# High weights times high and low input as one product of 512 columns in the MLPs

## The chip, the core and the metric

The kernel runs on one core of one Trainium2 chip. The metric is the device time of one execution in microseconds (us), the median over the runs of a kernel. Each core has a matrix engine (TensorE, PE in the rows, its weight loads as PEld), three engines for elementwise work (VectorE, DVE in the rows; ScalarE, ACT; GpSimd, POOL), and a queue (SP) that here issues the weight transfers. TensorE writes its products to an accumulator memory, PSUM: 8 banks of 512 fp32 values per partition, over 128 partitions.

## The reference, cut to what matters

Two layers over x of shape (1, 256, 2048). Each layer has a mixer (layer 0: a state-space part and a retention part; layer 1: latent attention) and then a gated MLP with a short convolution. The change touches the MLPs only:

```python
def conv_ffn(hn, w_up, conv_w, conv_b, w_down):
    a = hn @ w_up                       # 2048 -> 2 x 5632
    ap = jnp.pad(a, ((0, 0), (CONV_WIDTH - 1, 0), (0, 0)))
    a = ap[:, :-2] * conv_w[0] + ap[:, 1:-1] * conv_w[1] + ap[:, 2:] * conv_w[2] + conv_b
    gate, val = jnp.split(a, 2, axis=-1)
    return (jax.nn.silu(gate) * val) @ w_down
...
for layer in range(DEPTH):
    ...
    h = h + conv_ffn(rms_norm(h, ln_ffn[layer]), ffn_w_up[layer], ...)
```

All inputs and outputs are fp32.

## The kernel before, in words

**Split products.** Activations lie transposed, 128 features on the partitions and the T = 256 tokens along the row. A product with an fp32 weight matrix is made of three products in the reduced format fp32r (the rows print it as f32 on TensorE). Each operand is written as high part plus low part: `hi` is the weight rounded to fp32r by ScalarE (L370), `lo` is `raw - hi`, made by VectorE (L761). The input has both parts side by side in one row of 512: columns 0 to 255 high, columns 256 to 511 low (`XS` for the up projections, `YF` for the down projections). For each 128x128 weight tile the kernel adds up high weight by high input (L1548), high weight by low input (L1549) and low weight by high input (L1552), all into the first 256 columns of a PSUM bank:

```python
def by_high(bank, wh, x, first):
    mm(PS[:, bank, 0:T], wh, x[:, 0:T], start=first, stop=False)
    mm(PS[:, bank, 0:T], wh, x[:, T:2 * T], start=False, stop=False)
```

The second half of each such bank is not used. Every matmul instruction comes with its own weight load, also the second of two with the same weights.

**Pieces and steps.** Weights stream from memory through 4 `raw` slots; two pieces come with one transfer. A piece is the part of a transfer that is split at once into one of 4 slots of `hi` and `lo`. In an up projection a piece is 8 tiles (4 along k, 2 output tiles `ft`): first 16 high products, then 8 low ones (`std_piece`). A step is 4 pieces and fills a pair of banks, one per output tile. Two pairs of banks (`pair(e)`, banks 0 to 3) are used in turn. In a down projection a piece has 6 or 5 tiles of one output tile and a step is 8 pieces (`down`, L1783).

**An MLP** (`feed_forward`) goes through the hidden width in two halves. A half is 22 up steps in 11 blocks of two (first gate, then value columns), then 8 down steps. After a gate or value step VectorE takes the bank pair out, multiplies by the row norm and writes `apad` (`scale_banks`, L810), which frees the banks (`bank_free`). GpSimd convolves the gate columns. For the value columns ScalarE starts the convolution (L575) and VectorE ends it (L1140). ScalarE applies SiLU (L584), VectorE multiplies gate by value (`hid`, L1146), ScalarE rounds to `YF` high (L592), VectorE subtracts for `YF` low (L1154). After a down step VectorE adds the bank pair to the residual `H` (`add_residual`, L773).

**Order.** Each engine runs its own instruction list strictly in order and the lists are written out by hand; semaphores tie them. TensorE needs, before a piece, its `hi` (`hi_ready`), before the low products its `lo` (`lo_ready`), and before a step the pair of banks freed by the step two before. ScalarE may split piece p once piece p - 4 is done on TensorE (`piece_done`). On VectorE and ScalarE the steps of a block stand between the splits: in a block ScalarE and VectorE split the 4 pieces of the next step, and then VectorE takes out the banks of the step just done. The splits of the following pieces stand behind the convolution, SiLU and rounding of the block. In the last block of a half two of those splits stand between its parts. The first down step takes, for each of two output tiles, 6 and 5 of the first 11 rows of `YF` (pieces 0 to 3), and then 6 and 5 of the last 11 (pieces 4 to 7). So before its piece 5, the sixth, TensorE waits for `YF` low of the last block (`hl_ready`, L1792).

Of the kernel before, what the change touches and what calls it, by code (L numbers as in the profile page):

```python
# [20 lines left out]
P = 128  # L21
T = 256
# [14 lines left out]
SLOTS = 4  # L37
# [28 lines left out]
def build(nc, A, out):  # L66
# [6 lines left out]
    with ctx:  # L73
# [103 lines left out]
        XF = sb("XF", [P, KD, T], fp32, ffn)  # L177
        ffn.close()
# [145 lines left out]
        hl_ready = sem("hl_ready")  # L324

# [33 lines left out]
        def _(act):  # L359
# [197 lines left out]
            def feed_forward(layer, n, p0, e0):  # L557

                for half in range(2):
# [3 lines left out]

                    def up(r, j0, kinds, first, last=False):
                        q = p + 8 * j0
                        if first:
                            first_step(n, q + 4)
                        else:
                            splits(q + 4, 8, r)
                        splits(q + 8, 8, r, kinds)  # L570

# [182 lines left out]
        def _(dve):  # L754
# [13 lines left out]
            def add_residual(p_end, e, sp_, se, r, j0, n=None):  # L768
# [3 lines left out]
                h = H[:, 2 * j0:2 * j0 + 2, :] if r is None else H[:, ds(r * 4 + 2 * j0, 2), :]  # L772
                V.tensor_tensor(h, h, PS[:, b:b + 2, 0:T], ALU.add).then_inc(bank_free, 1)  # L773
# [32 lines left out]
            def scale_banks(d, p_end, e, sp_=0, r=None):  # L806
# [3 lines left out]
                V.tensor_tensor(d, PS[:, b:b + 2, 0:T], rn2, ALU.mult).then_inc(bank_free, 1)  # L810

# [304 lines left out]
            def feed_forward(layer, n, p0, e0):  # L1116
                for half in range(2):
# [4 lines left out]
                    def up(r, j0, kinds, first, last=False):  # L1122
# [8 lines left out]
                        scale_banks(apad[:, 0, :, 2:T + 2], q + 4, e + 2 * j0, 8, r)  # L1131
                        splits(q + 8, 8, r, kinds)
                        scale_banks(apad[:, 1, :, 2:T + 2], q + 8, e + 2 * j0 + 1, 8, r)
# [30 lines left out]
                    add_residual(q + 8, ed, 0, 0, None, 0, m)  # L1164
                    with dve.Fori(0, 3) as r:
                        for i in (1, 2):
                            splits(q + 8 * i + 4, 16, r, ("down",) * 8)
                            add_residual(q + 8 * i + 8, ed + i, 16, 2, r, i, m)
# [5 lines left out]
                    add_residual(q + 64, ed + 7, 0, 0, None, 7, m)  # L1174
# [364 lines left out]
        def _(pe):  # L1539
# [10 lines left out]

            def by_low(bank, wl, x, last):
                return mm(PS[:, bank, 0:T], wl, x[:, 0:T], start=False, stop=last)  # L1552
# [4 lines left out]
            def std_piece(p, i, bank, mov, s=0, r=None, nk=4, pieces=4):  # L1557

                pe.wait_ge(hi_ready, at(p + 1, s, r))
                for ft in range(2):  # L1560
                    for k in range(nk):
                        kk = i * nk + k
                        wh, _ = tile(p, k, nk, ft * P)
                        by_high(bank + ft, wh, mov(kk), kk == 0)
# [7 lines left out]
            def step(p, e, mov, s=0, se=0, r=None, before=None, after=None):  # L1572
# [3 lines left out]
                for i in range(4):  # L1576
                    if before:
                        before(i)
                    std_piece(p + i, i, pair(e), mov, s, r)
# [188 lines left out]
            def feed_forward(layer, n, p0, e0):  # L1768
                for half in range(2):
# [3 lines left out]
                    if half == 0:  # L1773
                        step(p, e, XSk, before=x_split(n), after=lambda i: norm_sum(n) if i == 2 else None)
                    else:
                        step(p, e, XSk)
                    step(p + 4, e + 1, XSk)
                    with pe.Fori(0, GS // 2) as r:
                        for j in range(4):
                            step(p + 8 + 4 * j, e + 2 + j, XSk, 16, 4, r)  # L1780
# [281 lines left out]
```

## Time and profile before

| what | value |
|---|---|
| median of 3 runs | 2176.58 us (2176.45 to 2183.63) |
| profiled execution, its own time | 2176.14 us |
| its span, first to last instruction | 2174.3 us |
| mean granted TensorE clock over the span | 0.997 |
| busy share: PE / DVE / ACT / POOL | 99% / 68% / 47% / 29% |
| matmul instructions | 18496 |
| memory read | 395.23 MB, 183 GB/s over the span |

How to read it: "busy" of TensorE is the time in which at least one matmul was in the pipeline, so 99% says that it hardly ever stood still, not that it ran at its peak. The other engines have room on average; what counts is whether their work is ready at the moment TensorE asks for it. In a timeline row the first number is the start in us from the span's start, the second the length in us, and the end of the row says how many instructions of the kind were merged. A single matmul lasts longer than the distance to the next one, because they overlap in the pipeline; the distance between starts is what it costs.

### The profile page before, as it was taken

How to read it: one execution, taken by the hardware profiler on the slowest of the kernel's cores; microseconds unless marked ns; L12 is line 12 of the kernel's file. 1: busy time of each engine (PE TensorE's matmuls, PEld its weight loads, DVE VectorE, ACT ScalarE, POOL GpSimd, SP SyncE). 2: the span in 40 equal slices, each digit the busy share in tenths (PEclk: the TensorE clock that was granted, in tenths of full speed). 3: DMA queues.
4: the chain of work that ended last, by engine and by line, in shares of the span. 5: the costliest groups of instructions: out<-in, count | busy, mean ns of one | idle time of the engine just before them, and what ended most of it. 6: DMA issues, size and time to landing. Idle time of an engine off the chain costs nothing.

```text
span 2174.3 us, 47266 instructions
## 1 busy us (share of the span) xinstructions
PE 2143.2 (99%) x18496; PEld 2120.6 (98%) x18496; DVE 1469.3 (68%) x1808; ACT 1028.0 (47%) x1338; POOL 632.7 (29%) x628
## 2 busy tenths in 40 slices
PE   8999999999999999999999999999999999999997
PEld 8999999999999999999999999999999999999997
DVE  6798895777666556666666667677665555666665
ACT  5455544444444444444444455445444444444443
POOL 4644430234343003434211111233434003343311
PEclk9999999999999999999999999999999999999999
DMA  6444444555554665555556444555554565555553
GB/s 256 176 161 160 159 170 144 200 191 199 187 199 152 210 212 194 197 189 197 169 190 227 145 141 143 186 186 196 194 192 170 191 208 206 192 194 190 168 197 118
DMA packets 67154, 399.91 MB, mean 184 GB/s; under 512 B 9776, under 2 KB 11696, under 8 KB 31600
## 3 DMA queue, kind: packets, MB, share of 16 engines
q1 hardware_dynamic: 60192, 391.15, 50.5%
q10 hardware_dynamic: 5712, 6.21, 0.9%
q8 instruction: 70, 1.15, 0.2%
q0 software_dynamic: 1152, 1.18, 0.2%
q14 instruction: 28, 0.23, 0.0%
HBM read 395.23 MB, written 2.10 MB: 183 GB/s over the span
## 4 chain that ended last, share of the span: by engine, by line
PE 94%; DVE 2%; ACT 1%; issue 1%; DVEq 1%; DMA 0%; POOL 0%; POOLq 0%; ACTq 0%
PE PS L1548 29%; PE PS L1552 29%; PE PS L1549 29%; PE PS L1707 1%; PE PS L1709 1%; PE PS L1708 1%; PE PS L1673 1%; DVE lo L761 1%; ACT hi L370 0%; PE PS L1914 0%; PE PS L1915 0%; PE PS L1928 0%; PE PS L1659 0%; PE PS L1901 0%; PE PS L1898 0%
## 5 line engine op out<-in xcount | busy, mean ns | idle before, releaser
L761 DVE TENSOR_TENSOR lo<-raw,hi 128x1024 fp32r<-128x1024 f32 (+2 forms) x826 | 950.5, 1170 | 498.5 <-ACT hi L370 493.5
L370 ACT ACTIVATE hi<-raw 128x1024 fp32r<-128x1024 f32 (+2 forms) x826 | 786.6, 970 | 744.2 <-PE PS L1552 700.1
L1548 PE MATMUL PS<-XS,hi 128*128 128x256 f32 x3600 | 847.5, 278 | 8.6 <-ACT hi L370 8.6
L1549 PE MATMUL PS<-XS,hi 128*128 128x256 f32 x3600 | 842.5, 277 | 0.0
L1548 PEld LDWEIGHTS PS<-XS,hi 128*128 128x128 f32 x3600 | 677.7, 188 | 11.9 <-issue 11.5
L1549 PEld LDWEIGHTS PS<-XS,hi 128*128 128x128 f32 x3600 | 677.4, 188 | 0.4
L1552 PE MATMUL PS<-XS,lo 128*128 128x256 f32 x3600 | 483.5, 277 | 0.0
L1552 PEld LDWEIGHTS PS<-XS,lo 128*128 128x128 f32 x3600 | 443.6, 188 | 0.0
L1549 PE MATMUL PS<-YF,hi 128*128 128x256 f32 x1408 | 331.8, 276 | 0.0
L1548 PE MATMUL PS<-YF,hi 128*128 128x256 f32 x1408 | 331.7, 276 | 0.0
L1497 POOL TENSOR_TENSOR ctmp<-apad,cws 128x512 f32<-128x512 f32 x88 | 131.9, 1520 | 524.7 <-DVE apad L810 524.7
L1548 PEld LDWEIGHTS PS<-YF,hi 128*128 128x128 f32 x1408 | 264.3, 188 | 0.0
L1549 PEld LDWEIGHTS PS<-YF,hi 128*128 128x128 f32 x1408 | 264.3, 188 | 0.0
L1552 PE MATMUL PS<-YF,lo 128*128 128x256 f32 x1408 | 201.2, 276 | 0.0
L1552 PEld LDWEIGHTS PS<-YF,lo 128*128 128x128 f32 x1408 | 178.6, 188 | 0.0
L1346 POOL TENSOR_TENSOR sq<-H 128x512 f32 x31 | 33.1, 1066 | 407.2 <-DVE H L773 407.2
L1140 DVE SCALAR_TENSOR_TENSOR cvo<-apad,cws,cvo 128x256 f32<-128x256 f32 x176 | 77.6, 482 | 50.5 <-ACT cvo L575 46.8
L1504 POOL TENSOR_TENSOR cvo<-cvo,ctmp 128x512 f32<-128x512 f32 x44 | 90.3, 2053 | 6.3
L1499 POOL TENSOR_SCALAR cvo<-apad,cws 128x256 f32<-128x256 f32 x88 | 91.5, 1047 | 0.0
L1492 POOL COPY cws<-cw 128x16 f32 (+1 forms) x44 | 10.9, 249 | 271.8 <-DVE hid L1146 251.9
L575 ACT ACTIVATE cvo<-apad,cws 128x256 f32<-128x256 f32 x88 | 48.2, 595 | 85.6 <-DVE apad L810 85.6
L592 ACT ACTIVATE YF<-hid 128x512 f32 (+1 forms) x44 | 27.9, 633 | 96.9 <-DVE hid L1146 96.9
(260 smaller groups left out, 2267.9 us busy)
## 6 DMA issues: line engine op xcount, KB each, us to landing
raw<-in_ffn_up SPq DMA_DIRECT2D x176, 1024.0 KB, 4.8
raw<-in_ffn_dn SPq DMA_DIRECT2D x128, 704.0 KB, 4.1
raw<-in_w_in SPq DMA_DIRECT2D x51, 1024.0 KB, 4.8
raw<-in_w_oe SPq DMA_DIRECT2D x16, 1024.0 KB, 4.8
raw<-in_w_oo SPq DMA_DIRECT2D x16, 1024.0 KB, 4.8
raw<-in_mla_dn SPq DMA_DIRECT2D x9, 1024.0 KB, 4.8
raw<-in_w_ukv SPq DMA_DIRECT2D x8, 1024.0 KB, 5.2
raw<-in_w_uq SPq DMA_DIRECT2D x8, 768.0 KB, 4.3
```

Source lines behind the costliest of these rows:

```text
L370: act.activation(hi[:, p % SLOTS, 0:n], raw[:, u % SLOTS, off:off + n], ACT.Copy).then_inc(hi_ready, 1)
L575: ins = act.activation(cvo[:, 1, t, :], apad[:, 1, t, 2:T + 2], ACT.Identity, bias=cws[:, 4 * t + 11:4 * t + 12], scale=cws[:, 4 * t + 10: ...
L592: act.activation(dh, hid[:, :, :], ACT.Copy).then_inc(hh_ready, 1)
L761: V.tensor_tensor(lo[:, p % SLOTS, 0:n], raw[:, u % SLOTS, off:off + n], f(hi[:, p % SLOTS, 0:n]), ALU.subtract).then_inc(lo_ready, 1)
L1140: V.scalar_tensor_tensor(out=cvo[:, 1, t, :], in0=apad[:, 1, t, i:T + i], scalar=cws[:, 8 + 4 * t + i:9 + 4 * t + i], in1=cvo[:, 1, t, :], ...
L1346: G.tensor_tensor(sq[:, :, :], h, h, ALU.mult)
L1497: G.tensor_tensor(ctmp[:, i, :, :], apad[:, 0, :, i:T + i], w(i), ALU.mult)
L1499: G.tensor_scalar(cvo[:, 0, t, :], apad[:, 0, t, 2:T + 2], cws[:, 4 * t + 2:4 * t + 3], cws[:, 4 * t + 3:4 * t + 4], ALU.mult, ALU.add)
L1504: G.tensor_tensor(cvo[:, 0], cvo[:, 0], ctmp[:, 0], ALU.add).then_inc(cv_ready, 1)
L1548: mm(PS[:, bank, 0:T], wh, x[:, 0:T], start=first, stop=False)
L1549: mm(PS[:, bank, 0:T], wh, x[:, T:2 * T], start=False, stop=False)
L1552: return mm(PS[:, bank, 0:T], wl, x[:, 0:T], start=False, stop=last)
```

## The change

In the up and down projections of both MLPs the two high products become one over all 512 columns of the input row, into the whole bank: columns 0 to 255 hold high by high, and, as before, low by high is added there; columns 256 to 511 hold high by low. The mixers keep the two products.

After an up step ScalarE copies the second halves of the two banks to a new buffer `low` (it waits for the step's last piece and for the previous banks to be free) and signals `half_ready`; VectorE adds the first halves to `low`, drains, and multiplies by the norm into `apad`. After a down step VectorE adds the second halves to `H`, drains, and then adds the first halves.

```diff
+        low = sb("low", [P, 2, T], fp32, ffn)
+                    def low_half(r, p_end, e_):
+                        act.wait_ge(piece_done, at(p_end, 8, r))
+                        act.wait_ge(bank_free, at(e_, 2, r))
+                        b = pair(e_)
+                        act.activation(low[:, :, :], PS[:, b:b + 2, T:2 * T], ACT.Copy).then_inc(half_ready, 1)
...
                             splits(q + 4, 8, r)
+                        low_half(r, q + 4, e + 2 * j0)
                         splits(q + 8, 8, r, kinds)
+                        low_half(r, q + 8, e + 2 * j0 + 1)
...
+                if wide:
+                    V.tensor_tensor(h, h, PS[:, b:b + 2, T:2 * T], ALU.add)
+                    dve.drain()
                 V.tensor_tensor(h, h, PS[:, b:b + 2, 0:T], ALU.add).then_inc(bank_free, 1)
...
+            def scale_halves(d, count, e, r):
+                dve.wait_ge(half_ready, at(count, 2, r))
+                b = pair(e)
+                V.tensor_tensor(low[:, :, :], low[:, :, :], PS[:, b:b + 2, 0:T], ALU.add)
+                dve.drain()
+                V.tensor_tensor(d, low[:, :, :], rn2, ALU.mult).then_inc(bank_free, 1)
...
-                        scale_banks(apad[:, 0, :, 2:T + 2], q + 4, e + 2 * j0, 8, r)
+                        scale_halves(apad[:, 0, :, 2:T + 2], 2 * (s0 + j0) + 1, e + 2 * j0, r)
                         splits(q + 8, 8, r, kinds)
-                        scale_banks(apad[:, 1, :, 2:T + 2], q + 8, e + 2 * j0 + 1, 8, r)
+                        scale_halves(apad[:, 1, :, 2:T + 2], 2 * (s0 + j0) + 2, e + 2 * j0 + 1, r)
...
+            def by_high_wide(bank, wh, x, first):
+                mm(PS[:, bank, :], wh, x, start=first, stop=False)
...
-                                by_high(pair(ed + i0) + ft, hi[:, pc % SLOTS, k * P:(k + 1) * P], YF[:, kk + k, :], kk + k == 0)
+                                by_high_wide(pair(ed + i0) + ft, hi[:, pc % SLOTS, k * P:(k + 1) * P], YF[:, kk + k, :], kk + k == 0)
```

`step` and `std_piece` take the function for the high products as an argument; all up steps of the MLPs pass `by_high_wide`, and the three `add_residual` calls of the MLPs (first down step, the six in a loop, the last) pass `wide`.

## Rows read from the trace of the kernel before

**Rows 1.** The page: engines' busy time (us, share of the span, instructions).
```profile
PE 2143.2 (99%) x18496; PEld 2120.6 (98%) x18496; DVE 1469.3 (68%) x1808; ACT 1028.0 (47%) x1338; POOL 632.7 (29%) x628
```

**Rows 2.** The page: the chain that ended last, by engine.
```profile
PE 94%; DVE 2%; ACT 1%; issue 1%; DVEq 1%; DMA 0%; POOL 0%; POOLq 0%; ACTq 0%
```

**Rows 3.** The waits of TensorE: us in total, times, longest; two longest and last of eleven.
```profile
PE PS L1548 <- ACT hi L370: 8.6, 1, 8.6
PE PS L1928 <- ACT C L679: 3.5, 7, 0.5
...
PE PS L1922 <- DVE C L1278: 0.4, 1, 0.4
```

**Rows 4.** Busy time by stretch, with TensorE clock and DMA share.
```profile
core 0: us, PE busy (x) PEld busy (x) DVE busy (x) ACT busy (x) POOL busy (x), PEclk, DMA share, GB/s
...
620.00:830.00 210.00, 210.00 (x1856) 210.00 (x1855) 121.98 (x140) 93.48 (x114) 34.64 (x28) 1.00 0.57 195
```

**Rows 5.** Groups by line over the MLPs of layer 0 (457 to 1175 us).
```profile
L1548 PE MATMUL PS<-XS,hi 128*128 128x256 f32 x1405 | 327.4, 276 | 0.0
...
L1548 PE MATMUL PS<-YF,hi 128*128 128x256 f32 x704 | 165.9, 276 | 0.0
```

**Rows 6.** Timeline, TensorE, steady stretch of an up projection (low products).
```profile
570.24 1.07 PE L1552 MATMUL PS<-XS,lo 128*128 128x256 f32 x8
...
572.96 1.07 PE L1552 MATMUL PS<-XS,lo 128*128 128x256 f32 x8
...
575.67 1.07 PE L1552 MATMUL PS<-XS,lo 128*128 128x256 f32 x8
```

**Rows 7.** Timeline, weight loads (PEld) beside products (PE).
```profile
500.42 0.28 PE L1548 MATMUL PS<-XS,hi 128*128 128x256 f32 x1
500.54 0.28 PE L1549 MATMUL PS<-XS,hi 128*128 128x256 f32 x1
500.65 0.28 PE L1548 MATMUL PS<-XS,hi 128*128 128x256 f32 x1
...
500.43 0.19 PEld L1549 LDWEIGHTS PS<-XS,hi 128*128 128x128 f32 x1
500.54 0.19 PEld L1548 LDWEIGHTS PS<-XS,hi 128*128 128x128 f32 x1
```

**Rows 8.** Timeline, weight loads of plain fp32 operands.
```profile
16.68 1.60 PEld L1610 LDWEIGHTS PS<-S,ones 128*128 128x128 f32 x8
```

**Rows 9.** The chain, start of the kernel: products of plain fp32 operands.
```profile
16.96 1.73 PE PS L1610 x8
```

**Rows 10.** Groups by line: nearest operations to the added ones.
```profile
L773 DVE TENSOR_TENSOR H<-H,PS 128x512 f32 x36 | 24.5, 680 | 0.0
...
L688 ACT ACTIVATE KN<-PS 128x512 f32<-128x512 f32 x8 | 4.8, 598 | 11.5 <-PE PS L1901 11.5
```

**Rows 11.** The instructions on apad: ns minimum, median, maximum.
```profile
L810 DVE TENSOR_TENSOR apad<-PS,rn x88: 677/683/685, 471.8 to 2041.2; 128x512 f32<-128x512 f32 x88
```

**Rows 12.** Timeline, ScalarE and VectorE in the steady block of rows 6.
```profile
573.27 2.94 ACT L370 ACTIVATE hi<-raw 128x1024 fp32r<-128x1024 f32 x3
...
568.14 0.68 DVE L810 TENSOR_TENSOR apad<-PS,rn 128x512 f32<-128x512 f32 x1
...
574.35 4.75 DVE L761 TENSOR_TENSOR lo<-raw,hi 128x1024 fp32r<-128x1024 f32 x4
```

**Rows 13.** Timeline, first block of layer 0: ScalarE, VectorE, then TensorE.
```profile
487.32 3.89 ACT L370 ACTIVATE hi<-raw 128x1024 fp32r<-128x1024 f32 x4
...
480.02 2.27 DVE L761 TENSOR_TENSOR lo<-raw,hi 128x1024 fp32r<-128x1024 f32 x1 [1.40 <-ACT hi L370]
...
488.40 3.50 DVE L761 TENSOR_TENSOR lo<-raw,hi 128x1024 fp32r<-128x1024 f32 x3 [0.26 <-ACT hi L370]
...
489.54 0.28 PE L1548 MATMUL PS<-XS,hi 128*128 128x256 f32 x1
```

**Rows 14.** Timeline, end of the first up projection: VectorE, then TensorE.
```profile
698.04 0.68 DVE L810 TENSOR_TENSOR apad<-PS,rn 128x512 f32<-128x512 f32 x1
...
704.85 0.69 DVE L1154 TENSOR_TENSOR YF<-hid,YF 128x512 fp32r<-128x512 f32 x1
...
705.10 0.84 PE L1552 MATMUL PS<-YF,lo 128*128 128x256 f32 x6
705.78 0.28 PE L1548 MATMUL PS<-YF,hi 128*128 128x256 f32 x1
```

**Rows 15.** Timeline, end of the kernel.
```profile
2159.29 0.69 DVE L773 TENSOR_TENSOR H<-H,PS 128x512 f32<-128x512 f32 x1 [5.82 <-PE PS L1552]
2160.01 0.63 ACT L736 ACTIVATE sums<-H 128x512 f32<-128x512 f32 x1 [7.41 <-DVE H L773]
```

More of the change, by code:

```diff
@@ L324, in build @@
         hl_ready = sem("hl_ready")
+        half_ready = sem("half_ready")
         odd_loads = sem("odd_loads")
@@ L766, in splits, with add_residual @@
                     split(p + i, s, r, k)
-            def add_residual(p_end, e, sp_, se, r, j0, n=None):
+            def add_residual(p_end, e, sp_, se, r, j0, n=None, wide=False):
                 dve.wait_ge(piece_done, at(p_end, sp_, r))
@@ L1163, in feed_forward @@
                     splits(q + 6, kinds=("down",) * 6)
-                    add_residual(q + 8, ed, 0, 0, None, 0, m)
+                    add_residual(q + 8, ed, 0, 0, None, 0, m, True)
                     with dve.Fori(0, 3) as r:
@@ L1167, in feed_forward @@
                             splits(q + 8 * i + 4, 16, r, ("down",) * 8)
[L1168 removed]
+                            add_residual(q + 8 * i + 8, ed + i, 16, 2, r, i, m, True)
                     splits(q + 60, kinds=("down",) * 4)
@@ L1173, in feed_forward @@
                         splits(q + 64, kinds=("std",) * 3)
-                    add_residual(q + 64, ed + 7, 0, 0, None, 7, m)
+                    add_residual(q + 64, ed + 7, 0, 0, None, 7, m, True)
                     if half == 1 and n < 3:
@@ L1555, in piece, with std_piece @@
                 pe.wait_ge(lo_ready, at(p + 1, s, r))
-            def std_piece(p, i, bank, mov, s=0, r=None, nk=4, pieces=4):
+            def std_piece(p, i, bank, mov, s=0, r=None, nk=4, pieces=4, high=by_high):
                 pe.wait_ge(hi_ready, at(p + 1, s, r))
@@ L1563, in std_piece @@
                         wh, _ = tile(p, k, nk, ft * P)
-                        by_high(bank + ft, wh, mov(kk), kk == 0)
+                        high(bank + ft, wh, mov(kk), kk == 0)
                 piece(p, s, r)
@@ L1570, in std_piece, with step @@
                 ins.then_inc(piece_done, 1)
-            def step(p, e, mov, s=0, se=0, r=None, before=None, after=None):
+            def step(p, e, mov, s=0, se=0, r=None, before=None, after=None, high=by_high):
                 if e >= 2:
@@ L1578, in step @@
                         before(i)
-                    std_piece(p + i, i, pair(e), mov, s, r)
+                    std_piece(p + i, i, pair(e), mov, s, r, high=high)
                     if after:
@@ L1773, in feed_forward @@
                     if half == 0:
-                        step(p, e, XSk, before=x_split(n), after=lambda i: norm_sum(n) if i == 2 else None)
+                        step(p, e, XSk, before=x_split(n), after=lambda i: norm_sum(n) if i == 2 else None, high=by_high_wide)
                     else:
-                        step(p, e, XSk)
-                    step(p + 4, e + 1, XSk)
+                        step(p, e, XSk, high=by_high_wide)
+                    step(p + 4, e + 1, XSk, high=by_high_wide)
                     with pe.Fori(0, GS // 2) as r:
                         for j in range(4):
-                            step(p + 8 + 4 * j, e + 2 + j, XSk, 16, 4, r)
+                            step(p + 8 + 4 * j, e + 2 + j, XSk, 16, 4, r, high=by_high_wide)
                     q, ed = p + UPP, e + 2 * GS
```

## The prediction

> **What bounds the kernel now.** First the page's busy times [rows 1]: TensorE is busy 99% of the span, VectorE 68%, ScalarE 47%. Then the chain that ended last [rows 2]: 94% of it is TensorE. A busy TensorE could still be one that waits in small gaps, so next its waits [rows 3]: eleven kinds, from one of 8.6 us at the very start down to 0.4, about 22 us together, and none of them more than one wait on a high or low product. In a down projection [rows 4] TensorE is busy for all of 210.00 us at a granted clock of 1.00, the upper level of 2.4 GHz, while the DMA engines are at 0.57. So the MLPs last as long as their matmul instructions stand apart, and the reader has to find that distance. The low products of consecutive pieces start at 570.24, 572.96 and 575.67 [rows 6]: 2.72 us for a piece of 24 instructions, 113.3 ns each. 256 columns at 2.4 GHz are 106.7 ns, so an instruction costs 6.7 ns over its columns.
>
> **What the change takes from TensorE.** The MLP of layer 0 has 1408 first high products on XS (three records are missing) and 704 on YF [rows 5]; layer 1 has the same. That makes 2 x 2112 = 4224 pairs that become one instruction each. A pair costs 2 x 113.3 = 226.7 ns now. The columns stay the same (213.3 ns), so the question is only what an instruction of 512 columns costs beyond them, and no row shows one. The bounds:
>
> - Nothing is won if the 6.7 ns go with the columns: 226.7 ns.
> - One fixed cost of 6.7 ns is won if it goes with the fp32r instruction: 220.0 ns.
> - More is won if the weight load sets today's distance. In the rows each weight load starts with the product before it, and the next product starts 0.11 us after the load [rows 7]: load and product take turns, both about 0.11 us long, and one cannot say from these rows which one waits. The nearest row with time to spare for the load are plain fp32 products near the start: 8 of them in 1.73 us, 216 ns each [rows 9], and their 8 loads are just as long (1.60 us for 8, the last one 0.19) [rows 8]. By their distance such an instruction keeps the array busy for twice its 256 columns, so 512 column times, and costs 3 ns over them.
>
> I take 216 ns. It is the only row where the array is held for 512 column times, and there the weight load of about 0.11 us is hidden as it would be here. Saved per pair 10.7 ns; times 4224 is 45.2 us. The other ends: 6.7 ns x 4224 = 28.2 us, and 0. The low products behind keep 113.3 ns. The last of them still hides the load for the next wide product.
>
> The Trainium skill says on "TensorE: Matmul & The Clock Gate", in "LDWEIGHTS (loading the stationary operand)", that a load takes its columns at 1.2 GHz. For 128 columns that is 106.7 ns, as an estimate, and it would make the load the slower part of today's turn; rows 7 do not contradict it. The same page's section "Back-to-back issue gap" gives N/2.4 + 2.5 ns for an isolated product, 109.2 ns for 256 columns and 215.8 for 512. The 113.3 ns of the trace do not agree with the first, the 216 ns of the fp32 rows agree with the second. By the page alone the pair would win 2.6 ns, and all of them 11 us.
>
> **What it adds, and where that lies.** An up step gets a ScalarE copy of 128x512 from PSUM (598 ns, L688) and a VectorE addition of 128x512 with one operand in PSUM (680 ns, L773) [rows 10]; the multiplication that follows now reads `low` and stays at about 683 ns [rows 11]. A down step gets one more addition of 680 ns. With a drain I count 0.75 us for VectorE each time (estimate: 0.68 plus 0.07, the step between two operations across a drain). The copy is hidden: it runs on ScalarE behind the split of the step's last piece, while VectorE subtracts that same piece for 1.2 us. In all VectorE gets 88 + 32 times 0.75 = 90 us more, ScalarE 88 x 0.60 = 53 us; at 68% and 47% that fits.
>
> What matters is latency at four places.
>
> - *The steady block.* The first split behind a block's convolution is ready at 574.35, where VectorE starts to subtract it; the chain of the block opens with the evacuation at 568.14 [rows 12]. TensorE wants that piece at 575.67 + 8 x 0.113 = 576.58 [rows 6]. Slack 2.2 us. From it go about 0.25 us for signal and weight load, 0.75 for the new addition, and 0.34 because TensorE runs 4 pieces of 8 pairs in between, 10.7 ns faster each. 0.9 us are left: nothing is paid.
> - *The first block of a layer.* A table load makes it later. The split is there at 488.40, TensorE starts it at 489.54 [rows 13]: 1.14 us. Less 0.25, 0.75 and 0.34 this is -0.2: 0.2 us of waiting, twice, 0.4 us.
> - *The end of an up projection.* The chain evacuation (698.04), convolution, SiLU, `YF` low ends at 704.85 + 0.69 = 705.54, and the piece that waits for it starts at 705.78 [rows 14]. The 0.24 us are just signal and weight load, so the slack is about nil. With 0.75 us more in the chain, and TensorE earlier by 28 pairs x 10.7 ns = 0.30 us, TensorE stands for 1.05 us. This comes four times: 4.2 us. What is late next is nothing: the splits of the following pieces shift with the chain and TensorE has stood by then.
> - *The end.* The last residual addition (2159.29, 0.69 us) is followed by the sum of squares (2160.01) that all of the final norm waits for [rows 15]: 0.75 us more. The other 31 residual additions lie beside 14 us of a down step, and the squares and the next layer's input have three pieces (8 us) of time.
>
> Sum: -45.2 + 0.4 + 4.2 + 0.75 = -39.9 us. Against the profiled execution's own 2176.14 us that is 2136.2; the median of the runs shown is 0.44 higher, so about 2137.
>
> **The rivals.**
>
> - *A fixed cost goes with each fp32r instruction* (220.0 ns). For it: the 6.7 ns are steady over every MLP piece, and the fp32 rows are of another format. Against it: it needs a cost twice as large as in the fp32 rows. Then 28.2 us are won; the stand at the end of an up projection is 0.75 + 0.19 = 0.94 us, four times 3.8, the first blocks cost 0.1, the end 0.75: 2176.6 - 23.6 = 2153.
> - *The cost goes with the columns, the change does not do what it says* (226.7 ns). Nothing is won, 0.75 us are lost at four ends and at the last: 3.75 us, 2180. Against it: 256 columns at 2.4 GHz explain 106.7 of 113.3 ns, and a rate of 2.26 columns a ns is neither clock level.
> - *VectorE's chain stops TensorE in every block.* This is the one on the slow side. The place is the first split behind each of 44 blocks; it decides from 1.65 us of added latency on (2.2 - 0.25 - 0.34). The row that speaks for it is a split stretched to 2.27 us where others take 1.2, at a time when GpSimd works [rows 13]. If the two new steps and the split before them all stretch by that 1.05 us, the chain grows by 0.75 + 3.15 = 3.9 us, TensorE stands 2.25 us in each block, 99 us, and the time is 2137 + 99 = 2236. It is slower than before by over 0.5% from about 2.8 us on. Against it: none of the 88 evacuations took over 685 ns [rows 11], and the new addition reads the same PSUM and writes as much.
> - *Products overlap beyond their columns.* The same page's section "Back-to-back issue gap" also gives about 131 ns for a sustained 512-column product. As a mechanism here: wide products would start before the columns of the one ahead are through. 226.7 - 131 = 95.7 ns x 4224 would take off up to 404 us before another engine stops it, at best 1772. No row here has 256 columns in less than 107 ns.
>
> **How the numbers follow.** 216 ns a pair: 0.67. 220 ns: 0.18. Columns: 0.08. VectorE's chain in every block: 0.04 with a loss, 0.02 with a part of the gain left. Overlap: 0.01. About 0.5%, 11 us, is what a measurement of this kernel can tell from no change, so the borders are 2165.7 and 2187.5. Faster: 0.67 + 0.18 + 0.02 + 0.01 = 0.88. Same: 0.08. Slower: 0.04. The predicted time is the likeliest case, 2137. Its own range is 2132 (no standing at the up ends) to 2142 (standing twice as long). The range given reaches to the 220 ns case, 2155, and holds 0.85.
>
> **What would show it.** In the trace after: wide products 0.216 us apart and a piece of an up projection in 8 x 0.216 + 8 x 0.113 = 2.63 us in place of 2.72; at 220 ns it is 2.67, at 226.7 it stays at 2.72. TensorE's waits should name four waits of about a microsecond on `YF` of L1154 at the first down step of each half, and two of a few tenths on the `hi` split in the first block of each layer. L810 should stay at 683 ns and the addition before it take 680. The final chain should be 0.75 us longer from the last product on. The prediction is wrong if the wide product takes another time than 216 ns, or if TensorE waits for `hi` in the blocks of the loops.

## The result and the profile after

The change makes the kernel slower: 2213.68 us median (2213.12 to 2220.03, 4 runs) against 2176.93 (2176.45 to 2183.63, 4 runs) on the same chip, ratio 1.0179, 95% interval 1.0165 to 1.0194. Forecast were 2137 us, a range of 2132 to 2155, and a chance of 0.04 for slower. The profiled execution has a span of 2211.3 us, at a mean granted TensorE clock of 0.996.

The page of the kernel after, busy times; it answers to [rows 1]:

```profile
PE 2175.3 (98%) x14272; PEld 1962.8 (89%) x14272; DVE 1575.6 (71%) x1928; ACT 1065.1 (48%) x1426; POOL 653.8 (30%) x628
```

The 4224 instructions are gone (18496 to 14272) and TensorE is busy 32 us longer. The waits of TensorE after (us in total, times, longest), two rows, against [rows 3]:

```profile
PE PS L1570 <- ACT hi L372: 8.3, 1, 8.3
...
PE PS L1574 <- ACT hi L372: 2.9, 4, 1.0
```

On the products of the MLPs only the four waits at L1574, the wide product, are new, 2.9 us together. The waits in the mixers and at the end differ by up to 1 us each. So the loss is not standing time. Busy time of the same stretch as [rows 4]:

```profile
core 0: us, PE busy (x) PEld busy (x) DVE busy (x) ACT busy (x) POOL busy (x), PEclk, DMA share, GB/s
620.00:830.00 210.00, 209.53 (x1204) 182.39 (x1203) 135.02 (x154) 97.02 (x122) 35.86 (x28) 1.00 0.55 190
```

The clock is at its upper level of 2.4 GHz (1.00), the DMA share is no higher than before. What is left is the distance between products. The timeline of TensorE in the steady stretch, against [rows 6] (L1574 the wide product, L1577 the low one):

```profile
566.58 2.02 PE L1574 MATMUL PS<-XS,hi 128*128 128x512 f32 x8
568.44 1.07 PE L1577 MATMUL PS<-XS,lo 128*128 128x256 f32 x8
569.35 2.02 PE L1574 MATMUL PS<-XS,hi 128*128 128x512 f32 x8
571.21 1.07 PE L1577 MATMUL PS<-XS,lo 128*128 128x256 f32 x8
572.12 2.02 PE L1574 MATMUL PS<-XS,hi 128*128 128x512 f32 x8
```

From 566.58 to 568.44 there are 8 wide products: 232.5 ns each, where the prediction took 216. The 8 low ones from 568.44 to 569.35 take 113.8 ns each. A piece lasts 2.77 us, where it was 2.72. The single starts in the trace show a pattern that comes back in nearly every piece of an up projection: 226, 236, 231, 236, 231, 236, 231, 236 ns, then 118 for the first low product and 113 to 114 for the rest. In the down projections it is mostly 233 to 234 in the pieces of six tiles and 226 to 236 in those of five. The low products behind are no longer at 113.3 ns either: their mean over the trace is 114.0 ns in the up projections and 116.4 in the down projections.

The two instructions that VectorE has in an up step after (ns minimum, median, maximum), against [rows 11]:

```profile
L832 DVE TENSOR_TENSOR apad<-low,rn x88: 691/693/1041, 471.4 to 2073.3; 128x512 f32<-128x512 f32 x88
```
```profile
L830 DVE TENSOR_TENSOR low<-low,PS x88: 672/677/682, 470.7 to 2072.5; 128x512 f32<-128x512 f32 x88
```

The addition is as forecast (680). The multiplication was thought to stay at 683 and is up to 1041 ns long. In the trace 24 of its 88 instances take 1023 to 1041 ns, and these are the 24 that lie beside an instruction of GpSimd; the other 64 take 691 to 694. Of the 88 additions 26 lie beside GpSimd, and they take 672 to 680 ns like the rest. VectorE in the steady block, against [rows 12]: split, addition, multiplication, and the first split behind the block; then the instruction of GpSimd that lies beside them:

```profile
567.87 1.22 DVE L772 TENSOR_TENSOR lo<-raw,hi 128x1024 fp32r<-128x1024 f32 x1 [1.27 <-ACT hi L372]
569.01 0.68 DVE L830 TENSOR_TENSOR low<-low,PS 128x512 f32<-128x512 f32 x1
569.76 1.03 DVE L832 TENSOR_TENSOR apad<-low,rn 128x512 f32<-128x512 f32 x1
...
576.31 1.23 DVE L772 TENSOR_TENSOR lo<-raw,hi 128x1024 fp32r<-128x1024 f32 x1
```
```profile
567.90 2.34 POOL L1526 TENSOR_TENSOR cvo<-cvo,ctmp 128x512 f32<-128x512 f32 x1
```

From the first step of the evacuation to that split it was 6.21 us (568.14 to 574.35), now it is 7.30 (569.01 to 576.31): 1.09 more, 0.75 for the addition and 0.34 for the longer multiplication. TensorE begins the piece at 577.67, 1.36 us after (it was 2.2): slack is left, nothing is paid there.

The end of the first up projection, VectorE and TensorE, against [rows 14]:

```profile
709.25 0.69 DVE L1176 TENSOR_TENSOR YF<-hid,YF 128x512 fp32r<-128x512 f32 x1
```
```profile
708.76 0.85 PE L1577 MATMUL PS<-YF,lo 128*128 128x256 f32 x6
710.08 1.40 PE L1574 MATMUL PS<-YF,hi 128*128 128x512 f32 x5 [0.47 <-ACT hi L372]
```

Six low products should take 0.69 us and took 1.32: TensorE stands for 0.63 us. The row names the split of ScalarE, but what came last is `YF` low (709.25 + 0.69 = 709.94, 0.14 us before the piece). This is one of the four waits above. The end of the kernel, against [rows 15]:

```profile
2194.31 0.69 DVE L785 TENSOR_TENSOR H<-H,PS 128x512 f32<-128x512 f32 x1 [6.02 <-PE PS L1577]
2195.07 0.69 DVE L787 TENSOR_TENSOR H<-H,PS 128x512 f32<-128x512 f32 x1
```

The second addition starts 0.76 us after the first.

**Where the 37 us are.** By the starts of products in the two traces, the up projection's second half (last product on `YF` to the next first one) lasts 244.18 us, was 239.47: 4.71 for 704 pairs. A down projection's half (first to last product on `YF`) lasts 123.4 or 124.0, was 119.57. Four up halves give 18.8 us and four down halves 16.5 (3.8 of it standing, as the experiment below shows by a down half of 122.75 without the new evacuation). The kernel's end, from the last product on `YF` to the last matmul, is 1.5 us longer. Together 36.8; the last matmul is 36.5 us later.

### The profile page after: what moved, and what is told of

Its sections match the earlier page's. It is cut to its first block, busy times and chain, and to the rows that moved or that the text cites. A ratio compares the mean times of both kernels' runs of the same rounds, so it can differ in the third digit from the quotient of the medians.

```text
span 2211.3 us, 39270 instructions
## 1 busy us (share of the span) xinstructions
PE 2175.3 (98%) x14272; PEld 1962.8 (89%) x14272; DVE 1575.6 (71%) x1928; ACT 1065.1 (48%) x1426; POOL 653.8 (30%) x628
## 3 DMA queue, kind: packets, MB, share of 16 engines
q10 hardware_dynamic: 5712, 6.21, 0.9%
## 4 chain that ended last, share of the span: by engine, by line
PE 93%; DVE 2%; ACT 2%; issue 1%; DVEq 1%; DMA 0%; POOL 0%; POOLq 0%; ACTq 0%
PE PS L1574 44%; PE PS L1577 28%; PE PS L1570 7%; PE PS L1571 7%; PE PS L1732 1%; PE PS L1734 1%; PE PS L1733 1%; DVE lo L772 1%; PE PS L1698 1%; ACT hi L372 1%; PE PS L1939 0%; PE PS L1940 0%; PE PS L1953 0%; PE PS L1684 0%; PE PS L1926 0%
## 5 line engine op out<-in xcount | busy, mean ns | idle before, releaser
L772 DVE TENSOR_TENSOR lo<-raw,hi 128x1024 fp32r<-128x1024 f32 (+2 forms) x826 | 969.5, 1197 | 419.7 <-ACT hi L372 415.8
L1574 PE MATMUL PS<-XS,hi 128*128 128x512 f32 x2816 | 712.8, 395 | 0.0
L1574 PEld LDWEIGHTS PS<-XS,hi 128*128 128x128 f32 x2816 | 503.2, 188 | 93.9
L1577 PEld LDWEIGHTS PS<-XS,lo 128*128 128x128 f32 x3600 | 471.8, 188 | 31.9
L1577 PE MATMUL PS<-XS,lo 128*128 128x256 f32 x3600 | 485.0, 277 | 0.0
L1574 PE MATMUL PS<-YF,hi 128*128 128x512 f32 x1408 | 369.2, 394 | 2.9 <-ACT hi L372 2.9
L1519 POOL TENSOR_TENSOR ctmp<-apad,cws 128x512 f32<-128x512 f32 x88 | 154.2, 1771 | 560.1 <-DVE apad L832 560.1
L1574 PEld LDWEIGHTS PS<-YF,hi 128*128 128x128 f32 x1408 | 245.5, 188 | 43.5 <-ACT hi L372 3.6
L1577 PEld LDWEIGHTS PS<-YF,lo 128*128 128x128 f32 x1408 | 201.3, 188 | 23.4
L1577 PE MATMUL PS<-YF,lo 128*128 128x256 f32 x1408 | 205.5, 279 | 0.0
L1570 PE MATMUL PS<-XS,hi 128*128 128x256 f32 x784 | 191.5, 285 | 8.3 <-ACT hi L372 8.3
L1571 PE MATMUL PS<-XS,hi 128*128 128x256 f32 x784 | 187.0, 280 | 0.0
L1570 PEld LDWEIGHTS PS<-XS,hi 128*128 128x128 f32 x784 | 148.8, 190 | 11.5 <-issue 11.2
L1571 PEld LDWEIGHTS PS<-XS,hi 128*128 128x128 f32 x784 | 148.8, 190 | 0.3
L1526 POOL TENSOR_TENSOR cvo<-cvo,ctmp 128x512 f32<-128x512 f32 x44 | 80.0, 1817 | 6.3
L1524 POOL TENSOR_TENSOR cvo<-cvo,ctmp 128x512 f32<-128x512 f32 x44 | 73.8, 1677 | 6.5
```

Of the source, the lines that this page charges most:

```text
L772: V.tensor_tensor(lo[:, p % SLOTS, 0:n], raw[:, u % SLOTS, off:off + n], f(hi[:, p % SLOTS, 0:n]), ALU.subtract).then_inc(lo_ready, 1)
L1519: G.tensor_tensor(ctmp[:, i, :, :], apad[:, 0, :, i:T + i], w(i), ALU.mult)
L1524: G.tensor_tensor(cvo[:, 0], cvo[:, 0], ctmp[:, 1], ALU.add)
L1526: G.tensor_tensor(cvo[:, 0], cvo[:, 0], ctmp[:, 0], ALU.add).then_inc(cv_ready, 1)
L1574: mm(PS[:, bank, :], wh, x, start=first, stop=False)
```

## The experiments

### Is it the wide product or the evacuation? A square of four

*Two products of 256 columns into the two halves, new evacuation* (`e1_two_halves`):

```diff
-                mm(PS[:, bank, :], wh, x, start=first, stop=False)
+                mm(PS[:, bank, 0:T], wh, x[:, 0:T], start=first, stop=False)
+                mm(PS[:, bank, T:2 * T], wh, x[:, T:2 * T], start=False, stop=False)
```

> The high products are two of 256 columns again, but into the two halves of the bank, and all of the new evacuation stays. Theory A (the 512-column product itself costs 226 to 236 ns, more than twice 113.3): products 113.3 ns apart as before, so 2177 plus the four stands at the ends of the up projections (0.75 us each) and 0.75 us at the end, about 2181. Theory B (the added copies and additions slow TensorE's stream, whatever its width): most of the 37 us stays, over 2205.

*Wide product, old evacuation* (`f1_wide_old_evac`). The second half of the bank is computed and never added:

```diff
-                        low_half(r, q + 4, e + 2 * j0)
...
-                        scale_halves(apad[:, 0, :, 2:T + 2], 2 * (s0 + j0) + 1, e + 2 * j0, r)
+                        scale_banks(apad[:, 0, :, 2:T + 2], q + 4, e + 2 * j0, 8, r)
...
-                    add_residual(q + 8, ed, 0, 0, None, 0, m, True)
+                    add_residual(q + 8, ed, 0, 0, None, 0, m)
```

> The wide products stay; the evacuation is that of the kernel before, and the second halves of the banks (high weight by low input) are never added. Theory A (the wide product itself costs 232.7 ns on average against 226.7 for two of 256): 4224 x 6 = 25 us over before and no stands at the ends of the up projections, about 2202, with the 226, 231 and 236 ns unchanged. Theory B (the later and heavier evacuation makes them slow): wide products at 226.7 or less throughout, about 2177.

*Both* (`f2_halves_old_evac`), the two edits together; it too never adds the second half:

> Two products of 256 columns into the two halves of the bank, evacuation as before, second halves never added. In the run with the new evacuation the products stood 113.3 ns apart in some halves and 117.6 in others; the change of rhythm came where a weight load had waited for its high weights, by then only 0.12 to 0.15 us ahead. Theory C (the late evacuation uses up the 2.3 us of slack, a load comes some ns late, and the stream stays in the slow rhythm): with the old evacuation the slack is back at 2.2 us, all products at 113.3 ns, 2177. Theory D (writing the second half of the bank brings the slow rhythm): stretches at 117.6 remain, over 2185.

| high products | evacuation | median us (runs) | ratio to before, 95% |
|---|---|---|---|
| wide | new (the change) | 2213.68 (4) | 1.0179 (1.0165 to 1.0194) |
| wide | old | 2210.50 (4) | 1.0148 (1.0131 to 1.0165) |
| two of 256 | new | 2199.85 (10, from 2187.66 to 2219.49) | 1.0102 (1.0068 to 1.0137) |
| two of 256 | old | 2176.81 (10, from 2174.43 to 2180.68) | 0.9996 (0.9985 to 1.0007) |

The wide product alone costs 2210.50 - 2176.81 = 33.7 us. In its trace the pattern of 226, 231 and 236 ns is unchanged, the up half is 244.18 us as in the change, the down half 122.75. Against two products of 256 columns (239.47 and 119.57 us) these are 4.71 us for 704 pairs, 6.7 ns a pair, and 3.18 us for 352, 9.0 ns a pair: about 6 ns on each wide product (mean 232.7), and the rest on the low products behind it. With the wide product the new evacuation adds 3.2 us; with two products of 256 it adds 23.0. The two costs don't add. The third row met neither of its forecasts (2181 and over 2205), its runs lie far apart, and it needs an explanation of its own.

### What of the wide product costs more than its columns?

Three experiments of one run each, with the new evacuation. *The same columns twice* (`e2_same_columns`): the wide product streams the 256 high columns two times (high by low is left out), so it reads a row of 1 KB and not of 2 KB.

```diff
-                mm(PS[:, bank, :], wh, x, start=first, stop=False)
+                xx = x[:, 0:T].unsqueeze(1).broadcast_to([P, 2, T])
+                mm(PS[:, bank, :].rearrange("p (a t) -> p a t", a=2), wh, xx, start=first, stop=False)
```

> The wide product streams the 256 high columns twice, so high weight by low input is left out. Theory A1 (the time goes with the columns that are streamed and written, not with what is read): wide products keep their 226, 231 and 236 ns, 2214. Theory A2 (reading a row of 2 KB is what is slow): they come down to about 226.7 or less, 2177 to 2190.

2215.29 us, distances unchanged (the same pattern, 232.5 ns in the steady stretch). Where the columns are read from is not it.

*Half the weights* (`e3_half_weights`): all wide products but the first of a bank use 64 weight columns (half of the outputs' high part is left out):

```diff
+                if first:
+                    mm(PS[:, bank, :], wh, x, start=first, stop=False)
+                else:
+                    mm(PS[0:64, bank, :], wh[:, 0:64], x, start=False, stop=False)
```

> All wide products but the first of each bank load 64 of 128 weight columns; the other half of their output is left out. Theory A3 (the weight load, which starts with each wide product, takes time from it): the load is half as long, and wide products come down from 232 towards 216 to 226 ns, a gain of 20 us or more against the kernel after, under 2195. Theory A1: no change of distance, 2214.

2218.4 us. The weight loads fall from 190 to 135 ns (two groups of its trace, 560 to 600 us), and the wide product stays at a mean of 231.9 ns (232.7 in the change), while the low ones of the up projections go from 114.0 to 116.8:

```profile
L1577 PEld LDWEIGHTS PS<-XS,hi 128*64 128x64 f32 x109 | 14.5, 135 | 8.0
L1575 PEld LDWEIGHTS PS<-XS,hi 128*128 128x128 f32 x6 | 1.1, 190 | 0.3
```

The length of the weight load is not it: with the load cut by 55 ns the wide product lost 0.8.

*384 and 128 columns* (`e4_384_128`), two products again:

```diff
+                mm(PS[:, bank, 0:384], wh, x[:, 0:384], start=first, stop=False)
+                mm(PS[:, bank, 384:512], wh, x[:, 384:512], start=False, stop=False)
```

> The 512 columns as a product of 384 and one of 128. If an fp32r product costs 17 column times for 16 columns (113.3 ns for 256, 226.7 for 512), the 384 columns take 170 ns and the 128 take 56.7 unless a weight load of about 110 ns sets the distance, which would make the pair 280 ns and the kernel about 2400 (2177 + 4224 x 0.053). If the load does not set it, 227 to 237 ns, 2180 to 2220.

2427.53 us, an up half of 280.54. Its timeline:

```profile
562.94 0.33 PE L1574 MATMUL PS<-XS,hi 128*128 128x384 f32 x1
563.11 0.22 PE L1575 MATMUL PS<-XS,hi 128*128 128x128 f32 x1
563.17 0.39 PE L1574 MATMUL PS<-XS,hi 128*128 128x384 f32 x1
563.40 0.22 PE L1575 MATMUL PS<-XS,hi 128*128 128x128 f32 x1
563.46 0.39 PE L1574 MATMUL PS<-XS,hi 128*128 128x384 f32 x1
```

The first 384 take 170 ns and the 128 behind them 60: they are near their columns at 2.4 GHz times 17/16 (170 and 56.7), like 256 in 113.3. So the 6.7 ns of an fp32r product do go with its columns. From then on a pair takes 0.29 us, 285 ns by the up half (227 and 58 more). The run had been forecast at 280 ns a pair and about 2400 us for the case that a weight load of about 110 ns does not fit behind a product of 128 columns, and it came out so: 113 + 170 = 283. That it is the load was not shown apart from this sum.

*Wide and low in turn* (`f3_interleaved`): each tile's wide and low product one after the other, new evacuation, in place of 8 wide ones and then 8 low ones.

```diff
+                        if high is by_high_wide:
+                            ins = by_low(bank + ft, wl, mov(kk), i == pieces - 1 and k == nk - 1)
```

> The kernel after, but each wide product is followed at once by the low product of the same tile, so no wide product follows another. The first wide product of each piece, which follows a low one, took 226 ns in the kernel after, the others 231 and 236. Theory E (the extra comes only where wide follows wide): wide 226.7, low 113 to 118, 4224 x 6 = 25 us less than the kernel after, 2185 to 2200. Theory F (every product over 256 columns pays it, whatever stands before): 230 to 236 stays, 2210 or more.

2246.79 us (4 runs), ratio 1.0316 (1.0299 to 1.0333). Now a wide product takes 235 ns and a low one 118 to 119:

```profile
563.10 0.28 PE L1577 MATMUL PS<-XS,lo 128*128 128x256 f32 x1
563.22 0.40 PE L1574 MATMUL PS<-XS,hi 128*128 128x512 f32 x1
563.46 0.28 PE L1577 MATMUL PS<-XS,lo 128*128 128x256 f32 x1
```

The edit also makes each piece of the up projections wait for its `lo` from the start; that is 2.7 us of waits in all. Changing the length at each step makes it worse, about 14 ns a pair over 17/16 of the columns in place of 6.7, so changes could be the cause of the whole extra. The next three test that, one run each. All have the old evacuation. *448 columns* (`g_448_columns`) and *320 columns* (`g_320_columns`) compute 64 and 192 columns of high by low less (what stands in the second half of a bank is not added in either):

```diff
-                mm(PS[:, bank, :], wh, x, start=first, stop=False)
+                mm(PS[:, bank, 0:448], wh, x[:, 0:448], start=first, stop=False)
```

> The wide product with the old evacuation, but over 448 of its 512 columns (64 columns of the high weights times the low input are left out). By columns x 17/16 at 2.4 GHz a product is 198.3 ns, 28.3 ns less than 226.7, so 4224 of them take 120 us off the 2176.8 of the two halves: 2057 us, and an up projection's half lasts 239.47 - 704 x 0.0283 = 219.5 us. If the extra 4 to 9 ns (226, 236, 231 in turn) come with every product longer than 256 columns, the distances are 198, 207, 203, the up half lasts 224 us and the time is about 2090. If they come only with a product that fills the bank (512), the distances are all 198 and the time is 2057.

> As the run with 448 columns, with 320 (192 columns of the high weights times the low input are left out). By the columns 141.7 ns a product. An up half of 239.47 - 704 x 0.085 = 179.6 us where nothing else stops TensorE, 184 us with 6 ns more for each product. VectorE, busy for about 1500 us, comes close to being late, so what is read here are the distances inside the pieces and not the total: all at 142 if only a full bank pays extra, 142 to 151 in turn if every product longer than 256 does. Total near 1820 if nothing waits, more where TensorE waits for the split.

*All products of the MLPs wide* (`g_all_wide`), the low one too; again the second half is not added:

```diff
+            def by_low_wide(bank, wl, x, last):
+                return mm(PS[:, bank, :], wl, x, start=False, stop=last)
```

> The wide product with the old evacuation, and the low product wide too (over both halves of the input; the second half of the bank is not read), so that the stream of the MLPs has products of one length only. If the extra nanoseconds come from the change of length between the wide and the low products, all stand 226.7 ns apart and the time is 2176.8 + 4224 x 0.1133 = 2655 us, an up half 239.47 + 704 x 0.1133 = 319.2 us. If each product of 512 columns costs 232.7 on the mean, it is 2655 + 8448 x 0.006 = 2706 us and an up half 327.7 us.

Timelines of the three, in this order (L1572 the high product, L1575 the low one, L1578 the wide low one):

```profile
564.87 1.78 PE L1572 MATMUL PS<-XS,hi 128*128 128x448 f32 x8
566.49 1.08 PE L1575 MATMUL PS<-XS,lo 128*128 128x256 f32 x8
567.41 1.78 PE L1572 MATMUL PS<-XS,hi 128*128 128x448 f32 x8
```
```profile
754.82 1.04 PE L1572 MATMUL PS<-YF,hi 128*128 128x320 f32 x6
755.70 0.87 PE L1575 MATMUL PS<-YF,lo 128*128 128x256 f32 x6
756.40 0.90 PE L1572 MATMUL PS<-YF,hi 128*128 128x320 f32 x5
```
```profile
562.95 2.03 PE L1578 MATMUL PS<-XS,lo 128*128 128x512 f32 x8
564.82 2.03 PE L1572 MATMUL PS<-XS,hi 128*128 128x512 f32 x8
566.68 2.03 PE L1578 MATMUL PS<-XS,lo 128*128 128x512 f32 x8
568.55 1.79 PE L1572 MATMUL PS<-XS,hi 128*128 128x512 f32 x7
```

448 columns: 1.62 us for 8, 202.5 ns, 4 over the 198.3 that 17/16 of the columns give; 2087.21 us, an up half of 223.63. The forecast of an extra for every length above 256 (224 us, about 2090) was right. 320 columns: 0.88 us for 6, 146.7 ns, 5 over the 141.7, with the low products at 116.7. The total there, 1958.95 us, is set by something else: TensorE waits 44 times for the `hi` split, 72.9 us in all, and in eleven stretches of the MLPs, 37.5 us together, its granted clock is 0.50. All wide: 5.60 us for 24, 233.3 ns each in every stretch of the MLPs; 2712.08 us where 2706 was forecast for this case and 2655 for the other. A stream of one length has 6.7 ns over 226.7 on every product, so the extra of the long product does not need a change of length. Changes add to it: the pair has 6.7 ns over 17/16 of its columns where the length changes every 8 products, 9.0 in the shorter pieces of the down projections, and about 14 where it changes each time.

### Why does the new evacuation cost 23 us with products of 256 columns?

The trace of `e1_two_halves` has no more waits than the change's, but a long stretch in which each product takes 117.7 ns and not 113.3. Low products of consecutive pieces, before and after the switch:

```profile
598.52 1.07 PE L1578 MATMUL PS<-XS,lo 128*128 128x256 f32 x8
```
```profile
657.10 1.10 PE L1578 MATMUL PS<-XS,lo 128*128 128x256 f32 x8
659.93 1.11 PE L1578 MATMUL PS<-XS,lo 128*128 128x256 f32 x8
662.76 1.10 PE L1578 MATMUL PS<-XS,lo 128*128 128x256 f32 x8
```

The last two steps are 2.83 us for 24 products, 117.9 ns (117.6 to 117.7 by the single starts); the step from 598.52 to the next low products (601.24) is 2.72, as before. The slow rhythm holds from 618.5 us on, and an up half in it lasts 248.86 us against 239.47. It sets in at one place. A stand of TensorE of 0.3 us at 707.4 us does not end it, one of 0.6 us at 1081 us does. VectorE, GpSimd, ScalarE, then TensorE where it sets in:

```profile
608.88 2.25 DVE L772 TENSOR_TENSOR lo<-raw,hi 128x1024 fp32r<-128x1024 f32 x1 [1.24 <-ACT hi L372]
611.05 0.67 DVE L830 TENSOR_TENSOR low<-low,PS 128x512 f32<-128x512 f32 x1
611.80 1.03 DVE L832 TENSOR_TENSOR apad<-low,rn 128x512 f32<-128x512 f32 x1
```
```profile
608.76 1.28 POOL L1524 TENSOR_TENSOR cvo<-cvo,ctmp 128x512 f32<-128x512 f32 x1
610.18 2.10 POOL L1526 TENSOR_TENSOR cvo<-cvo,ctmp 128x512 f32<-128x512 f32 x1
```
```profile
617.27 1.99 ACT L372 ACTIVATE hi<-raw 128x1024 fp32r<-128x1024 f32 x2
```
```profile
618.47 0.29 PE L1574 MATMUL PS<-XS,hi 128*128 128x256 f32 x1
618.59 0.28 PE L1575 MATMUL PS<-XS,hi 128*128 128x256 f32 x1
618.71 0.28 PE L1574 MATMUL PS<-XS,hi 128*128 128x256 f32 x1
```

The split in front of the evacuation takes 2.25 us in place of 1.22 and the multiplication 1.03 in place of 0.69, so with the addition the chain is late by 1.03 + 0.34 + 0.75 = 2.1 us, the whole slack. The `hi` that TensorE needs is ready at 618.33 (617.27 and 1.06 for one split), just when its weight load is due: the loads before are 113 ns apart and this one comes after 125, at 618.37. From the product at 618.47 on the starts are 0.12 us apart. No wait is listed. Two experiments ask whose lateness it is, and whether lateness alone does it.

*ScalarE's copy only* (`g_scalar_copy_only`): the copy and the wait for it stay, and VectorE multiplies out of PSUM as before (high by low is left out in the up steps; the down steps keep both additions):

```diff
-                V.tensor_tensor(low[:, :, :], low[:, :, :], PS[:, b:b + 2, 0:T], ALU.add)
-                dve.drain()
-                V.tensor_tensor(d, low[:, :, :], rn2, ALU.mult).then_inc(bank_free, 1)
+                V.tensor_tensor(d, PS[:, b:b + 2, 0:T], rn2, ALU.mult).then_inc(bank_free, 1)
```

> Two products of 256 columns into the two halves of a bank (2199.85 us with the whole new evacuation, 2176.8 with none), with ScalarE's copy and the wait for it kept in the up steps, but VectorE evacuating as before, one multiplication out of PSUM (the high weights times the low input are left out of the up steps; the down steps keep their addition). If VectorE's added step and its multiplication out of SBUF beside GpSimd's work are what made the split late, the slack behind a block is back near 2 us, the products keep 113.3 ns and the time is 2177 to 2181 us. If the copy or the wait for it is, the slack stays below 1 us and the time is near 2200.

2179.55 us (2175.38 to 2181.55, 10 runs), ratio 1.0012 (1.0002 to 1.0021). Its steady block, from evacuation to split:

```profile
567.40 0.68 DVE L830 TENSOR_TENSOR apad<-PS,rn 128x512 f32<-128x512 f32 x1
...
573.61 3.50 DVE L772 TENSOR_TENSOR lo<-raw,hi 128x1024 fp32r<-128x1024 f32 x3
```

6.21 us again, the slack back at 2.27, all MLP products at 113.3 ns, and an up half of 239.47. So the copy, the wait for it and the 32 additions of the down steps cost 2.6 us (0.4 to 4.6), and about 20 of the 23 are VectorE's added step and its multiplication out of SBUF. The two were not taken apart.

*A late ScalarE* (`f4_late_scalar`): the kernel before with four idle copies on ScalarE in each block, in front of the split:

```diff
+                        for k in (4, 5, 6):
+                            act.activation(PS[:, k, :].rearrange("p (a n) -> p a n", a=4), ones[:, :].unsqueeze(1).broadcast_to([P, 4, P]), ACT.Copy)
+                        act.activation(idle[:, :, :], ones[:, :].unsqueeze(1).broadcast_to([P, 4, P]), ACT.Copy)
```

> The kernel before with four idle ScalarE copies of 128x512 behind each of the 44 blocks of the up projections, which use up about 2.1 of the 2.27 us that the next high weights are ready ahead. Its products and its evacuation are untouched. Theory C (a weight load that comes some ns late turns the stream to the slow rhythm): stretches of products at 117.6 ns in the MLPs where the kernel before has none, up to 12672 x 4.3 ns = 54 us, 2185 to 2230. Theory D (the rhythm has nothing to do with waiting): 113.3 throughout and at most the waits themselves, below 2187.

2201.35 us. The split is ready 0.05 us before the piece is due and the up halves take 243.1 and 244.7 us. Most blocks pay in a gap; at 577.42 it is one product of 0.23 us:

```profile
577.42 0.38 PE L1552 MATMUL PS<-XS,hi 128*128 128x256 f32 x1
577.65 0.28 PE L1553 MATMUL PS<-XS,hi 128*128 128x256 f32 x1
```

The slow rhythm comes too (918 to 942 us and 1851 to 1898 us in this trace), but not behind most late splits; in `e1_two_halves` too the second layer keeps 113.3 ns with splits only 0.12 us early. So a late split can cost time with hardly a wait listed, and it can start the slow rhythm; it does not do so each time. What decides that stays open.

## Why the prediction was wrong, point by point

- **"I take 216 ns"**: this step failed, and with it the sum. The wide product measured 232.5 ns. Of this, 226.7 is the rival "the cost goes with the columns", which had a chance of 0.08 and a time of 2180 us: 128, 256 and 384 columns take 57 to 60, 113.3 and 170 ns. The rest, 6 ns on the mean, was in no rival; it comes with products of 320, 448 and 512 columns, except the first of a piece in the mixed stream. The 216 ns row was of plain fp32 [rows 9], the product of another format, 2.7 ns over the time that the prediction gives its columns and not 1/16. The prediction named this difference and took the row all the same, because it was the only one of 512 column times. The saving of 45.2 us became a loss of 33.7, 78.9 us apart. Result and forecast are 76.7 apart; the evacuation makes up the rest, 3.2 us where 5.35 was forecast.
- **"The low products behind keep 113.3 ns"**: this was put at nothing without a row, and failed too. They take 114.0 and 116.4 ns on the mean, about 6 us in all (2816 x 0.6 ns and 1408 x 3.1 ns).
- **The argument against the rival** (that 2.26 columns a ns is neither clock level) was no evidence. A rate need not be a clock level. Rows of the kernel before that the prediction did not use show that the 6.7 ns are not always there: at a granted clock of 0.50 fp32r products of 256 columns start 213.3 ns apart (65.30 to 68.50 us, 15 steps), which is their columns at 1.2 GHz with nothing over.
- **The Trainium skill**, "TensorE: Matmul & The Clock Gate", section "Back-to-back issue gap", gives N/2.4 + 2.5 ns for an isolated product, by which 512 columns would be 215.8 ns (an estimate from that formula), and about 131 sustained. No trace here agrees with either for fp32r: 226 to 236 ns in the mixed stream, 233.3 in the uniform one.
- **Overlap** (1772 us): did not occur; no product came under its columns.
- **The four ends of up projections**, 1.05 us each: there, at the place named, 3.8 us where 4.2 was forecast. That the sum came so near is in part luck. Of each 1.05 us 0.30 were for a TensorE that comes earlier, and it came later. The stands are 0.7 us at the first half's end and 1.2 at the second's, where the split in front of the evacuation takes 1.55 us in place of 0.83, beside GpSimd, which was in no term. **The end**, 0.75: the added addition is 0.76; the stretch from the last `YF` product is 1.5 longer (8.1 us against 6.6), but it takes 6.8 to 7.6 us in runs with the old evacuation, so about half of that is not the change's.
- **The first blocks**, 0.2 us twice: no wait, and 1.0 us of slack in the second layer. TensorE was not earlier by 0.34 us but later.
- **The steady block**: no wait in the change, as forecast, but the latency was mis-sized: 1.09 us, and up to 2.1 where GpSimd works beside the split, against 0.75. The "against" of the rival on VectorE's chain read [rows 11], an operation with one operand in PSUM; the new multiplication has both in SBUF, and it stretches to 1041 ns. `e1_two_halves` shows the price that this has when the products are as short as before: 23 us at the median, 11 to 43 in single runs. In the change itself the split in front of the evacuation was not stretched in the same way and the slack stayed at 0.7 to 1.5 us behind the blocks of the loops; only the ends are left, 3.2 us. Why GpSimd's work meets that split in the one and not in the other was not tried.
- The Trainium skill, "SBUF — State Buffer", section "SBUF: two separate sides", says that VectorE with two SBUF inputs and GpSimd take turns at one pair of ports, each holding it for a whole instruction. The trace agrees: L832 took 1023 to 1041 ns beside GpSimd and 691 to 694 elsewhere, and the addition L830, one operand in PSUM, 672 to 682 in either case. None of the 88 L810 of the kernel before (677 to 685) lay beside an instruction of GpSimd, so their even times alone were no evidence.
- **Copy hidden on ScalarE**: right, `g_scalar_copy_only`.

No version tried that adds all three products beats the kernel before. Of the forms measured, two products of 256 columns are the cheapest here, as long as they stay in the rhythm of 113.3 ns.

A reading of the prediction that is not right, without weight in the sum: the stretch of [rows 4] is not a down projection alone, since the down projection starts at 696 us in that trace; 620 to 696 us belongs to the up projection.

## What to carry to other kernels

Price an instruction from rows of its own format: a column count says little where fp32r and fp32 differ in their cost per column. Joining two products saves nothing if the cost goes with the columns, and fewer instructions and idle weight loads (PEld from 98% to 89%) are no gain in themselves. When an operand moves from PSUM to SBUF on VectorE, ask what GpSimd does at that moment, and keep more slack for TensorE's input than the listed waits suggest.

## What the runs showed of the hardware

- At a granted clock of 1.00 an fp32r product takes about 17/16 of its columns at 2.4 GHz: 57 to 60 ns for 128 columns, 113.3 for 256, 170 for 384 (one at the head of a piece). In a stream of longer ones 4 to 7 ns come on top: 320 columns 146.7, 448 columns 202.5, 512 columns 232.5 (mixed) or 233.3 (uniform). Excluded as the cause of the extra are the source of the columns, the length of the weight load, a full bank, the evacuation, and the change of length. What it is stays open.
- At a granted clock of 0.50 neither shows: 213.3 ns for 256 columns (kernel before, 65.30 to 68.50 us) and 266.7 for 320 (`g_320_columns`, 487.3 to 488.9 us), just their columns at 1.2 GHz. So what adds the 1/16 and the extra is seen only at the upper level.
- A stream of 256-column fp32r products has two rhythms, 113.3 and about 117.7 ns, at the same granted clock. The kernel before has the second in its mixers alone (81.86 to 84.68 us: 2.82 us for 24), the MLPs run in the first. A slow stretch lasted 462 us in `e1_two_halves`, 24 and 47 us in `f4_late_scalar`.
- Beside an instruction of GpSimd a VectorE operation with both operands in SBUF can be stretched (the 128x512 multiplication: 691 to 694 ns alone, 1023 to 1041 beside it; the 128x1024 split: 1.21 to 1.23 us alone and up to 2.31 beside it), the 26 additions with an operand in PSUM that lie beside one were not (672 to 680).
